# The rotary rotation of queries, index queries and keys: 32-row copies on ScalarE in place of TensorE matmuls

## What is computed

```
def apply_rope(x, cos, sin):
    x1, x2 = jnp.split(x.astype(jnp.float32), 2, axis=-1)
    ...
    return jnp.concatenate([x1 * c - x2 * s, x2 * c + x1 * s], axis=-1).astype(x.dtype)
...
        q_c = apply_rope(a_q.reshape(a_shape), cos, sin)
        k_c = apply_rope(a_k.reshape(a_shape), cos, sin)
        qi = apply_rope(a_qi.reshape(B, S, IDX_HEADS, IDX_DIM), cos, sin)
        ki = apply_rope(a_ki[:, :, None, :], cos, sin)[:, :, 0, :]
        y_c = dsa_attention(q_c, k_c, a_v.reshape(a_shape), qi, ki, a_w).reshape(B, S, D_BRANCH)
```

## Time and profile before

| | us |
|---|---|
| median of 3 runs | 1720.02 |
| lowest, highest | 1719.49, 1720.11 |
| the profiled execution, its time | 1718.21 |
| its span in the trace | 1716.3 |
| TensorE busy (matmuls) | 1616.0 |
| VectorE busy | 1300.1 |
| ScalarE busy | 951.9 |
| GpSimd busy | 43.2 |

### The profile page before, as it was taken

One profiled execution on the slowest core, in us unless ns is written; L12 is line 12 of the kernel. 1 busy time (PEld: TensorE's weight loads), 2 busy tenths in 40 slices (PEclk: granted clock), 3 DMA queues, 4 the chain that ended last, 5 costly groups with the idle time before them and its releaser, 6 DMA issues.

```text
span 1716.3 us, 28017 instructions
## 1 busy us (share of the span) xinstructions
PE 1616.0 (94%) x11632; PEld 1508.1 (88%) x11632; DVE 1300.1 (76%) x1567; ACT 951.9 (55%) x990; POOL 43.2 (3%) x43
## 2 busy tenths in 40 slices
PE   3998999999997988999999997799999999999998
PEld 3898999999997988999999997698899788888886
DVE  6699676676666699677676667885895788898886
ACT  5647454554444646555454444554553677777774
POOL 0100001000000010001000000000000000000000
PEclk9999999999998999999999999899999899999999
DMA  7444535555555444535555555254445499999993
GB/s 204 148 123 131 165 123 172 166 190 182 180 183 143 147 124 134 162 123 172 171 187 187 178 184 158 74 172 123 123 148 190 168 358 352 362 352 369 353 353 130
DMA packets 222399, 328.92 MB, mean 192 GB/s; under 512 B 20832, under 2 KB 179168, under 8 KB 222304
## 3 DMA queue, kind: packets, MB, share of 16 engines
q1 hardware_dynamic: 222304, 327.56, 57.8%
HBM read 326.49 MB, written 1.05 MB: 191 GB/s over the span
## 4 chain that ended last, share of the span: by engine, by line
PE 77%; DVE 15%; issue 3%; ACT 3%; DMA 1%; POOL 0%; SPq 0%; DVEq 0%; ACTq 0%
PE bank L2021 23%; PE bank L2022 23%; PE bank L2023 23%; DVE w_lo L1197 2%; ACT w_hi L697 1%; DVE work L1249 1%; DVE work L1354 1%; PE bank L2375 1%; DMA w_raw<-in_w_in 1%; DVE w_lo L1650 1%; PE bank L2481 1%; DVE work L1679 1%; DVE work L1302 1%; DVE work L1372 1%; PE bank L2534 1%
## 5 line engine op out<-in xcount | busy, mean ns | idle before, releaser
L1197 DVE TENSOR_TENSOR w_lo<-w_raw,w_hi 128x2048 fp32r<-128x2048 f32 x158 | 362.7, 2296 | 138.9 <-ACT w_hi L697 138.2
L2021 PE MATMUL bank<-act_h,w_hi 128*128 128x256 f32 (+1 forms) x1408 | 408.7, 290 | 27.9 <-DVE act_l L1233 9.5
L2023 PE MATMUL bank<-act_h,w_lo 128*128 128x256 f32 (+1 forms) x1408 | 399.8, 284 | 0.0
L2022 PE MATMUL bank<-act_l,w_hi 128*128 128x256 f32 (+1 forms) x1408 | 399.7, 284 | 0.0
L697 ACT CAST w_hi<-w_raw 128x2048 fp32r<-128x2048 f32 x158 | 300.5, 1902 | 43.0 <-PE bank L2023 34.3
L2021 PEld LDWEIGHTS bank<-act_h,w_hi 128*128 128x128 f32 x1408 | 269.6, 191 | 36.8 <-issue 31.8
L2022 PEld LDWEIGHTS bank<-act_l,w_hi 128*128 128x128 f32 x1408 | 269.8, 192 | 0.6
L2023 PEld LDWEIGHTS bank<-act_h,w_lo 128*128 128x128 f32 x1408 | 269.2, 191 | 0.0
L2022 PE MATMUL bank<-u_l,w_hi 128*128 128x256 f32 x768 | 217.3, 283 | 0.0
L2023 PE MATMUL bank<-u_h,w_lo 128*128 128x256 f32 x768 | 216.9, 282 | 0.0
L2021 PE MATMUL bank<-u_h,w_hi 128*128 128x256 f32 x768 | 215.9, 281 | 0.0
(11 more groups left out here) (446 smaller groups left out, 2911.8 us busy)
## 6 DMA issues: line engine op xcount, KB each, us to landing
w_raw<-in_w_in SPq DMA_DIRECT2D x88, 1024.0 KB, 5.5
w_raw<-in_ffn_up SPq DMA_DIRECT2D x48, 1024.0 KB, 5.2
w_raw<-in_e_gate SPq DMA_DIRECT2D x26, 1024.0 KB, 7.1
w_raw<-in_ffn_down SPq DMA_DIRECT2D x24, 1024.0 KB, 5.0
w_raw<-in_e_up SPq DMA_DIRECT2D x23, 1024.0 KB, 7.1
w_raw<-in_e_down SPq DMA_DIRECT2D x23, 1024.0 KB, 7.3
w_raw<-in_w_out SPq DMA_DIRECT2D x16, 1024.0 KB, 5.2
w_raw<-in_w_branch SPq DMA_DIRECT2D x12, 1024.0 KB, 5.1
```

The source lines that it names most:

```text
L1197: V.tensor_tensor(w_lo[c % RING][:], w_raw[c % RING][:], w_hi[c % RING][:].bitcast(F32), ALU.subtract).then_inc(sem[f"lo_ready{c % RING}"], 1)
L2021: mm(out, a_hi, b_hi, start=first, stop=False, skip_group_check=True)
L2022: mm(out, a_hi, b_lo, start=False, stop=False, skip_group_check=True)
L2023: return mm(out, a_lo, b_hi, start=False, stop=last, skip_group_check=True)
```

## The change

The matmuls with `rot` go. ScalarE writes each evacuated pair twice: first as four 32-row copies that exchange the halves of each head, straight from the bank into `rope_sin`, then as the plain copy to `rope_in` as before. The index key gets two such copies into `ki_sin`. The sign goes into the table of sines: at the start VectorE adds up the columns of `rot` to get plus or minus one for each row, and multiplies the table by it. VectorE now multiplies `rope_sin` by the sines in place. Since the swapped copies overwrite `rope_sin[n % 2]`, ScalarE waits for VectorE's addition of the pair two before (`rope_done`) where it used to wait for TensorE (`rope_turned`).

```diff
-    rope_cos=6, rope_turned=7, rope_done=7, idx_done=6, idx_relu=6, idx_used=6, mask_ready=2,
+    rope_cos=6, rope_swap0=3, rope_swap1=3, rope_done=7, idx_done=6, idx_relu=6, idx_used=6, mask_ready=2,
...
+            def swap_halves(dst, src, first_rows):
+
+                for r in first_rows:
+                    own(nc.scalar.copy(dst[r:r + 32], src[r + 32:r + 64]))
+                    ins = nc.scalar.copy(dst[r + 32:r + 64], src[r:r + 32])
+                    if r < first_rows[-1]:
+                        own(ins)
+                return ins
...
                         need(act, "rope_cos", L, n - 1)
-                        need(act, "rope_turned", L, n if n > 2 else 1)
+                        need(act, "rope_done", L, n if n > 2 else 1)
+                    swap_halves(rope_sin[n % 2], ps, (0, 64)).then_inc(sem[f"rope_swap{n % 2}"], 1)
                     ins = nc.scalar.copy(rope_in[n % 2], ps)
...
                     own(nc.scalar.copy(rope_ki[64:128, :], psum[6][64:128, 0:T]))
+                    own(swap_halves(ki_sin, psum[6][:, 0:T], (64,)))
...
-                k = 1 if i == 0 else i + 2
-                need(dve, "rope_turned", L, k)
-                own(V.tensor_tensor(rope_sin[i % 2], psum[6 + i % 2][:].rearrange("p (b t) -> p b t", b=2),
+                need(dve, f"rope_swap{i % 2}", L, i // 2 + 1)
+                own(V.tensor_tensor(rope_sin[i % 2], rope_sin[i % 2],
                                     sin_t[:].unsqueeze(1).to_broadcast([P, 2, T]), ALU.mult))
...
-                need(dve, "rope_turned", L, 2)
+                need(dve, "rows_ready", L, 1)
                 up = slice(64, 128)
-                own(V.tensor_tensor(ki_sin[up, :], psum[7][up, 0:T], sin_t[up, :], ALU.mult))
+                own(V.tensor_tensor(ki_sin[up, :], ki_sin[up, :], sin_t[up, :], ALU.mult))
...
+            dve.wait_ge(sem["zeros_ready"], 1)
             step(V.tensor_copy(tmp, pos))
+            step(V.reduce_sum(half_sign, rot, AX_X))
+            step(V.tensor_scalar(half_sign, half_sign, -1.0, None, ALU.mult))
...
-                V.tensor_scalar(table[:], tmp, pi_below, None, ALU.min).then_inc(sem["setup_dve"], 1)
+                V.tensor_scalar(table[:], tmp, pi_below, ones_col if quarter else half_sign, ALU.min, ALU.mult)\
+                    .then_inc(sem["setup_dve"], 1)
...
-            def turn_pair(L, i):
-
-                need(pe, "evac_act", L, 2 + i + 1)
-                if i >= 2:
-                    need(pe, "rope_done", L, i if i > 2 else 2)
-                for b in range(2):
-                    ins = mm(psum[6 + i % 2][:, b * T:b * T + T], rot, rope_in[i % 2][:, b, :],
-                             start=True, stop=True)
-                ins.then_inc(sem["rope_turned"], 1)
-
...
-                if c == 5:
-                    need(pe, "rows_ready", L, 1)
-                    turn_pair(L, 0)
-                    mm(psum[7][64:128, 0:T], rot[64:128, 64:128], rope_ki[64:128, :], start=True, stop=True)\
-                        .then_inc(sem["rope_turned"], 1)
-                if 6 <= c <= 10:
-                    if c == 6:
-                        need(pe, "rope_done", L, 2)
-                    if c == 8:
-                        need(pe, "a_row", L, 1)
-                        need(pe, "lru_i", L, 1)
-                    turn_pair(L, c - 5)
                 if c == 8:
+                    need(pe, "a_row", L, 1)
+                    need(pe, "lru_i", L, 1)
```

More of the change, by code:

```diff
@@ L1621, in _ @@
             pos = work[:, 0:T].bitcast(I32)
+            half_sign, ones_col = tiny[:, 858:859], ones[:, 0:1]
             ang, turns, tmp = work[:, T:2 * T], work[:, 2 * T:3 * T], work[:, 3 * T:4 * T]
```

## The result

| | before | after |
|---|---|---|
| median, us | 1719.76 | 1733.46 |
| lowest, highest of 4 runs | 1719.29, 1720.11 | 1731.57, 1735.41 |
| the profiled execution, its time | 1718.21 | 1731.57 |
| its span in the trace | 1716.3 | 1729.8 |

The ratio is 1.0082 (95% interval 1.0069 to 1.0094): the change makes the kernel slower by 13.7 us. The forecast was 1730.8 us, 1724 to 1741.

What follows compares the result with a forecast made beforehand. VectorE's unbroken run of about 65 us per layer was taken as the bound. Layers +5.24 and +4.70 us and clock +0.9 made 10.8 on 1718.21, 1729.0; the median's 1.8 more gave 1730.8 us, range 1724 to 1741.

Steps and rivals of the forecast that it cites:

- The frame: Between 73.47 and 138.79 us VectorE's unbroken run paces each layer, so 21.2 us less of TensorE's time gives nothing.
- Start: Copies of chunks 4 and 5 delay the cast VectorE needs at 76.87 us: +2.96 us in the first layer.
- the bound that I called dear: Upper bound on a 32-row ScalarE copy, 0.60 us each instead of 0.48, each paying its full 0.59.
- New waits: ScalarE's wait for VectorE's addition delays later casts: VectorE waits +1.80 us at chunk 7, none at 8, +0.97 at 9.
- The key and the setup: Key's two copies and setup's extra VectorE work fall in idle time: nothing; uncovered, under 1 us a layer and 0.6 once.
- GpSimd: Its products start later: old collisions with VectorE give back 2.14 us in the first layer, new ones add 1.65.
- Clock: Longer TensorE idling before chunk 14 makes both layers' stage to the softmax go like the first: +0.9 us.
- The sum: First layer 5.24 us, second 4.70, together +9.9; with 0.9 for the clock 10.8 us.
- TensorE's time coming back: Rival: VectorE's run shortens too, TensorE sets the pace and 21.2 us go: 1699 us; chance 0.04.
- Only the start: Rival: waits at chunks 7 and 9 are hidden, 5.3 us more, 1725 us; chance 0.15.
- The clock rival: TensorE, idle before chunks 8, 9 and 10, runs slower and holds up ScalarE's evacuation: 12 more, 1743 us; chance 0.10.
- The lock on the sine product: Rival: GpSimd holds each of twelve edited L1298 products up to 1.32 us: 16 us, 1747 us; chance 0.03.

Runs made afterwards that it cites:

- the kernel without rotation: Changed kernel without any swapped copies, the sine product reading the unrotated pair, so neither rotation matmuls nor copies: 1721.09 us, ratio 1.0009.
- the wait alone: Kernel before, with ScalarE's evacuation of chunks 6 to 9 also waiting for VectorE's addition of the pair two before: 1721.44 us, ratio 1.0012.
- the copies alone: Kernel before, rotation matmuls kept, plus four 32-row copies into unused scratch ahead of each pair's plain copy, no new wait: 1727.52 us, ratio 1.0047.
- the probes: Two kernels without rotation, four scratch copies of varied rows and starts ahead of each pair's plain copy: starts 0.48 or 0.60 us apart; no total time given.
- swaps behind the cast: Changed kernel with the four swapped copies read from rope_in and placed, with their wait, behind the step's cast: 1728.88 us, ratio 1.0053.
- swaps where ScalarE has time: Changed kernel with six buffers, copies behind the casts, the first two pairs' later still, VectorE's first rope behind its gate rows: 1722.06 us, ratio 1.0012.

## Why the prediction was right, and where it was off

**The frame held.** That the removed matmuls give nothing back is shown by the kernel without rotation beside the wait alone. That VectorE's run sets the end, and ScalarE's cast is what it gets late, is shown by the three bracketed rows and by the copies alone.

**Start.** Forecast +2.96 us, measured +3.98. The mis-sized term is the distance from copy to copy: I took 0.48 us from a 128-row copy with a cast behind it, and it is 0.60, the bound that I called dear. Two pairs make 0.96 of the missing 1.02. The reason that I gave for that bound (each pays its full length) isn't the right one; the changed first row is. The estimate from the Trainium skill's page "VectorE: DVE Perf Modes" (section on the TRN2 errata), 2.28 us a pair, was nearer to the measured 2.40 than my 1.92, but not for its reason: it is the length of a copy, and the length is 0.58 us in the probes' rows of 0.48 us from start to start too. With 0.60 in the prediction's own sum the forecast would have been 1734.6 us, against 1733.46 measured.

**New waits.** At chunks 7 and 9, none at chunk 8, as forecast: +1.80 and +0.97 forecast, +2.29 and +1.44 measured, 0.49 and 0.47 more. A pair's copies are 0.48 us longer, which is all of it. The wait alone showed that without the copies this wait costs 2.1 us in all, with other collisions and no idle time.

**The key and the setup.** Both were put at nothing, and that held. The key's two copies stand at 62.16 and 62.55 us, in idle time, and chunk 4's first copy comes at 66.25 us (66.36 before). The setup's second lower half is 0.55 us late (17.79 us; the transfer that the setup waits for landed 0.50 us later in this trace), and by VectorE's row at 61 us only 0.10 us of that is left (61.28 against 61.18 us); it is part of the 3.98.

**GpSimd.** Gone: −2.14 forecast, −2.20 measured (L1308's 1.03 against 0.42 us is 0.61, not the 0.55 in the prediction's sum). New: +1.65 forecast, +1.53 measured, but not where I had put them. The index-row reciprocal met a product (87.64 us) and kept its 1.74 us; the scans and chunk 9's lower half weren't stretched; a four-row gate operation and the recurrence's last product were. The products of chunks 7 and 9 (100.38 and 118.22 us) fell mostly into VectorE's new idle time. The size came out by luck more than by working. The edited sine product (L1307) took 0.68 to 0.69 us everywhere, since no product ran beside it.

**Clock.** Forecast +0.9 us, measured −0.9 in the first layer and −0.1 in the second. The step that failed is "with a longer gap I expect both layers to go like the first": the gap before chunk 14 didn't grow (3.06 to 3.07 us, and 2.06 in the second layer), and both layers went like the second, 27.12 and 27.05 us. Stretches of both kernels, with the granted clock behind the busy times, first of before, then of after:

```profile
138.00:167.00 29.00, 26.22 (x194) 25.70 (x195) 27.18 (x53) 20.90 (x35) 0.00 (x0) 0.88 0.48 145
```

```profile
145.00:174.00 29.00, 25.16 (x201) 24.85 (x202) 28.14 (x53) 21.21 (x35) 0.00 (x0) 0.94 0.49 145
```

The granted share of that stage rose from 0.88 to 0.94; in the second layer it is 0.94 in both kernels (661 to 690 us before, 675 to 704 after). The gap's length doesn't decide it: both layers before have 3.06 us of idle and a first matmul of 0.55 and 0.35 us; the wait alone has 3.05 us of idle, 0.36 us, and 27.06 us for the stage; the copies alone 3.13, 0.55 and 27.86. What does decide it stays open.

**The sum.** The steps of the two layers were 9.9 us forecast and 14.2 measured (7.12 and 7.04). The clock took back 1.0 of it instead of adding 0.9, 0.8 came up between the layers and 0.5 went behind the second. That is 13.5 against the forecast 10.8: 2.7 us under, inside the range, since two errors of opposite sign partly cancel.

**The rivals.** TensorE's time coming back fell with the kernel without rotation. "Only the start" fell with the second and third bracket, and even without those two the copies alone cost 8.2 us, not 5.3. The clock rival was right about the clock and wrong about its price. Stretches of both kernels, first of before, then of after:

```profile
92.00:116.00 24.00, 23.58 (x188) 21.55 (x187) 23.48 (x29) 13.13 (x14) 3.91 (x3) 1.00 0.43 132
```

```profile
92.00:116.00 24.00, 13.66 (x81) 11.64 (x80) 21.19 (x28) 13.95 (x19) 2.75 (x2) 0.73 0.33 97
```

TensorE idles there for long with the change and its granted share falls from 1.00 to 0.73, between the two levels (0.63 to 0.80 in stretches of 8 us). This fits with the busy time, which fell by only 4.8 of the 13.4 us of matmuls removed, though I didn't count the longer matmuls one by one. It held up nothing: ScalarE's first copies at chunks 6 to 9 all wait for VectorE's addition and none for a bank, VectorE's idle rows are all put down to ScalarE's cast, and terms of 7.04 us account for the 7.12. The lock on the sine product didn't come to pass; as no product met it, whether it would be held up wasn't tested.

## What to carry to other kernels

Work taken from an engine that waits anyway was worth nothing here, and work given to an engine that stands one step ahead of the pacing one costs what its queue delays, not its busy time: the same 48 copies cost 13.7 us at the head of ScalarE's step, 8.6 us behind the cast, and 1.8 us where nothing that VectorE waits for stood behind them (with six buffers and VectorE's order changed to allow it). Cost a short instruction by the distance between starts, in a row of its own kind; where row ranges alternate, that distance is longer. Before moving anything by a microsecond, list what runs on GpSimd: each of its products costs VectorE up to 1.1 us if it meets an operation of two SBUF inputs, and some of one (a copy, a product with a constant) too.

## What the runs showed of the hardware that I had not expected

- ScalarE's copies of 512 columns out of a bank have the same length for 32, 64 or 128 rows (0.58 to 0.59 us), and start 0.48 us apart if they begin at the same rows, 0.60 us if source or destination begins at another row than in the copy before.
- The same four copies from SBUF start 0.64 us apart (70.39 and 71.03 us with the swaps behind the cast), each 0.61 to 0.62 us long. Copies from SBUF that begin at the same rows weren't tried.
- A GpSimd product stretches VectorE's operations on four rows as much as those on 128: 0.41 to 1.06 us, and seven of them from 3.09 to 4.21. Scans are stretched too, 2.44 to 3.42 us. So are operations with one SBUF input: a copy of 64 rows from 0.29 to 1.30 us (swaps behind the cast), a product with a constant on four rows from 0.28 to 1.29 (swaps where ScalarE has time). The reciprocal on four rows isn't: 1.74 us beside the product at 87.64 us in the changed kernel, as before.
